# Expert rows of a mixture-of-experts layer: stored and gathered at the end, or added to the output by indirect DMAs

## The reference

```python
# router: 4 groups x 8 experts; each token takes the 2 best of its best group
gate = softmax(top_logit) * g_w[:, None]
flat_e = g_idx[:, None] * 8 + top_idx
# each expert: the tokens that chose it, in blocks padded with a row of zeros
def run_block(xblk, e):
    hid = silu(xblk @ w1[e]) * (xblk @ w3[e])        # 1024 -> 512
    return hid @ w2[e]                               # 512 -> 1024
y[slot_tok] += yb * slot_w[:, None]                  # weighted, two experts a token
out = x + y
```

## Time and profile before

| | us |
|---|---|
| median of 3 runs (1937.62 to 1944.29) | 1937.9 |
| the profiled execution's own time | 1937.75 |
| its span in the trace | 1935.9 |
| PE busy | 1719.5 (89%) |
| PEld busy | 1246.5 (64%) |
| DVE busy | 1138.3 (59%) |
| ACT busy | 893.8 (46%) |
| POOL busy | 796.3 (41%) |

### The profile page before, as it was taken

The page is one execution under the profiler, slowest core; times in us unless marked ns, Lnnn a source line. Parts: engine busy times, 40 slices in busy tenths (PEclk is TensorE's granted clock), DMA queues, the critical chain, the costliest instruction groups (busy, mean ns, idle before and its releaser), DMA issues.

```text
span 1935.9 us, 22760 instructions
## 1 busy us (share of the span) xinstructions
PE 1719.5 (89%) x7364; PEld 1246.5 (64%) x7364; DVE 1138.3 (59%) x1523; ACT 893.8 (46%) x1196; POOL 796.3 (41%) x388
## 2 busy tenths in 40 slices
PE   1888999989999899989689998873999999999993
PEld 1766878777878688458577467662566656666562
DVE  4667865472232346335553314225899998998995
ACT  3534433443224122123321134331888888888882
POOL 0476977333424144104202031100566556665663
PEclk9899999999999899999859999885999999999997
DMA  8344435222242213412104232122999999999995
GB/s 287 115 121 124 129 118 184 88 97 93 76 147 88 109 40 123 165 66 82 67 1 128 87 131 87 44 87 85 337 395 396 393 389 389 396 391 395 389 370 189
DMA packets 138669, 357.94 MB, mean 185 GB/s; under 512 B 12661, under 2 KB 64125, under 8 KB 113768
## 3 DMA queue, kind: packets, MB, share of 16 engines
q1 hardware_dynamic: 130264, 325.32, 46.1%
q10 hardware_dynamic: 4544, 18.88, 2.5%
q0 software_dynamic: 3792, 12.85, 2.1%
HBM read 333.95 MB, written 23.07 MB: 184 GB/s over the span
## 4 chain that ended last, share of the span: by engine, by line
PE 48%; issue 19%; POOL 14%; DVE 11%; DMA 4%; ACT 2%; SPq 1%; POOLq 0%; DVEq 0%; ACTq 0%
PE ps L720 11%; PE ps L721 11%; PE ps L722 11%; PE ps L692 10%; POOL parts L2284 9%; PE ps L702 3%; POOL idx L2294 2%; DMA ring<-in_w_in 1%; DVE act_parts L1671 1%; POOL parts L2250 1%; PE ps L928 1%; PE ps L901 1%; POOL arena L2297 1%; DMA ring<-in_w_out 1%; DMA arena<-in_sgu_b 1%
## 5 line engine op out<-in xcount | busy, mean ns | idle before, releaser
L2250 POOL TENSOR_TENSOR parts<-ring,parts 128x1024 fp32r<-128x1024 f32 x150 | 371.0, 2480 | 808.1 <-ACT parts L1087 805.3
L1366 ACT CAST parts<-ring 128x1024 fp32r<-128x1024 f32 x384 | 396.2, 1048 | 90.9 <-PE ps L722 67.2
L720 PE MATMUL ps<-parts,act_parts 128*128 128x512 f32 (+2 forms) x1088 | 427.8, 393 | 7.1 <-DVE parts L2074 2.2
L721 PE MATMUL ps<-parts,act_parts 128*128 128x512 f32 (+2 forms) x1088 | 423.7, 389 | 0.0
L722 PE MATMUL ps<-parts,act_parts 128*128 128x512 f32 (+2 forms) x1088 | 423.2, 389 | 0.0
L2074 DVE TENSOR_TENSOR parts<-ring,parts 128x1024 fp32r<-128x1024 f32 x289 | 394.3, 1415 | 26.0 <-ACT parts L1366 19.3
L2284 POOL TENSOR_TENSOR parts<-ring,parts 128x1024 fp32r<-128x1024 f32 x95 | 264.1, 2781 | 235.8 <-ACT parts L1366 235.2
L1087 ACT CAST parts<-ring 128x1024 fp32r<-128x1024 f32 x150 | 155.6, 1047 | 409.4 <-PE ps L722 288.5
L720 PE MATMUL ps<-act_parts,parts 128*128 128x512 f32 x640 | 253.9, 397 | 20.4 <-POOL parts L2250 15.6
L721 PE MATMUL ps<-act_parts,parts 128*128 128x512 f32 x640 | 251.0, 392 | 0.0
L722 PE MATMUL ps<-act_parts,parts 128*128 128x512 f32 x640 | 250.9, 392 | 0.0
(11 more groups left out here) (248 smaller groups left out, 1824.3 us busy)
## 6 DMA issues: line engine op xcount, KB each, us to landing
ring<-in_w SPq DMA_DIRECT2D x192, 1024.0 KB, 7.6
ring<-in_w_in SPq DMA_DIRECT2D x30, 1024.0 KB, 7.3
ring<-in_w_in SPq DMA_DIRECT2D x34, 512.0 KB, 5.6
ring<-in_w_ada SPq DMA_DIRECT2D x12, 1024.0 KB, 11.4
ring<-in_w_ret_out SPq DMA_DIRECT2D x8, 1024.0 KB, 10.8
ring<-in_w_out SPq DMA_DIRECT2D x8, 1024.0 KB, 9.7
y_rows<-arena ACTq DMA_DIRECT2D x32, 256.0 KB, 6.4
ring<-in_w_in SPq DMA_DIRECT2D x16, 256.0 KB, 4.0
```

What stands on the lines that cost most here:

```text
L720: pe.matmul(o, lhs[1], rhs[0], start=start, stop=False)
L721: pe.matmul(o, lhs[0], rhs[1], start=False, stop=False)
L1366: act.copy(parts[:, n % 4, 0, :], ring[:, j, n % 4 * 1024:(n % 4 + 1) * 1024]).then_inc(piece_hi, 1)
L2250: pool.tensor_tensor(parts[:, g % 4, 1, :], ring[:, st.place(j), k * 1024:(k + 1) * 1024], parts[:, g % 4, 0, :].bitcast(F32), ALU.subtrac ...
```

## The change

1. **Add in place of store.** `y_blk` is no longer stored by ScalarE. GpSimd adds it to `out` with an indirect DMA that accumulates (`add_to_out`), with the tokens of the block's slots as rows of the destination. `out` is first filled with `x` by one 2 MB store of SP behind that of `h3_rows`. Block c's add has to land (`added`) before GpSimd starts the next turn of the loop and before VectorE may write `y_blk` again (`y_blk_free`).
2. **Weights where the up products meet.** A fifth routing product makes `slot_w`, the weight of each slot, and `hidden` multiplies by it.
3. **Padded slots are skipped.** An empty slot now holds 2048, which is over the bound (511), so gather and add leave its row out. The first slot of a block keeps token 0 when it is empty.
4. **Gone**: the stores to `y_rows`, its clearing, the eight gathers at the end, VectorE's eight operations on them, and the four stores of `out`.
5. **GpSimd's loop** is peeled by one turn, and `add_to_out` and `added` are put into it.

```diff
@@ end of SP's and ScalarE's part
-            sp.wait_ge(zero_ready, 1)
-            ... (4 MB of zeros to the spare rows of y_rows, and the waits on it)
             sp.dma_start(h3_rows.rearrange("(m p) d -> p m d", p=P), h3_tok).then_inc(h3_stored, 16)
+            sp.dma_start(out_v, x).then_inc(out_done, 16)
...
-            for m in range(MT):
-                sp.wait_ge(x_ready, 3 + m + 1)
-                sp.dma_start(out_v[:, m, :], x[:, m, :]).then_inc(out_done, 16)
-            sp.wait_ge(out_done, MT * 16)
+            sp.wait_ge(out_done, 16)
+            sp.wait_ge(y_added, steps * 16 + 16)
+            sp.nop().then_inc(settled, 1)
...
                 up("moe", r + 2, 4, r + 1, ends=("moe", 1, r + 1))
-                store_rows(r)
                 down(r + 1)
@@ TensorE, before its wait for the first gather
+            pe.wait_ge(block_w_ready, 1)
+            filled("route", 4, product(bank("route", 4)[0:SLOTS, 0:64], [slot_oh[:, q, :] for q in range(2 * MT)],
+                                       [block_w[:, q, :] for q in range(2 * MT)]))
@@ VectorE
-            own(dve.tensor_copy(slot_tok[:, :], full("route", 3)[0:SLOTS, 0:64]))
+            o = full("route", 3)[0:SLOTS, 0:64]
+            own(dve.tensor_scalar(slot_tok[:, :], o, float(SKIPPED), None, ALU.add))
+            own.wait()
+            own(dve.tensor_scalar(slot_tok[0:1, :], slot_tok[0:1, :], SKIPPED - 1, None, ALU.bitwise_and))
             own.wait()
             drained("route", 3, dve.nop())
             dve.nop().then_inc(slots_ready, 1)
+            for c in range(2 * MT):
+                own(dve.tensor_scalar(block_w[:, c, :], cst("iota"), blkf[:, c:c + 1], w01[:, c:c + 1], ALU.is_equal, ALU.mult))
+            own.wait()
+            dve.nop().then_inc(block_w_ready, 1)
+            own(dve.tensor_copy(slot_w[0:SLOTS, :], full("route", 4)[0:SLOTS, 0:64]))
...
             def add_rows(c):
-                dve.wait_ge(y_stored, (c + 1) * 16)
+                dve.wait_ge(y_blk_free, c + 1)
...
             def hidden(stage, b, i=0):
-                moe(dve.tensor_tensor(hid[0:SLOTS, :], full(stage, 2, i)[0:SLOTS, :], t_h[0:SLOTS, :], ALU.mult))
+                moe(dve.scalar_tensor_tensor(out=hid[0:SLOTS, :], in0=full(stage, 2, i)[0:SLOTS, :], scalar=w,
+                                             in1=t_h[0:SLOTS, :], op0=ALU.mult, op1=ALU.mult))
@@ GpSimd
-            pool.wait_ge(conv_ready, KT)
-            pool.memset(zeros, 0.0).then_inc(zero_ready, 1)
...
-                pool.indirect_dma_start(xg[0:SLOTS, :], None, h3_rows,
-                                        bass.IndirectOffsetOnAxis(ap=idx[:, 0:1], axis=0)).then_inc(xg_in, 16)
+                pool.indirect_dma_start(xg[0:SLOTS, :], None, h3_rows, bass.IndirectOffsetOnAxis(ap=idx[:, 0:1], axis=0),
+                                        bounds_check=S - 1, oob_is_err=False).then_inc(xg_in, 16)
+
+            def add_to_out(c):
+                pool.wait_ge(y_sum_ready, c + 1)
+                pool.tensor_copy(idx_out[:, :], slot_tok[:, bass.ds(c, 1)]).then_inc(idx_out_ready, 1)
+                pool.wait_ge(idx_out_ready, c + 1)
+                pool.nop().then_inc(settled, 1)
+                pool.indirect_dma_start(out[0], bass.IndirectOffsetOnAxis(ap=idx_out[:, 0:1], axis=0), y_blk[0:SLOTS, :], None,
+                                        bounds_check=S - 1, oob_is_err=False, compute_op=ALU.add).then_inc(y_added, 16)
+
+            def added(c):
+                pool.wait_ge(y_added, (c + 1) * 16)
+                pool.nop().then_inc(y_blk_free, 1)
...
-            with pool.Fori(0, steps) as r:
-                turned("moe", r)
-                gather(r + 2)
-                for n in (3, 7, 11):
-                    low(n, r * 12 + (8 + n))
-            ... (the eight gathers of y_rows)
+            turned("moe", 0)
+            gather(2)
+            for n in (3, 7, 11):
+                low(n, 8 + n)
+            pool.wait_ge(out_done, 16)
+            pool.nop().then_inc(y_blk_free, 1)
+            with pool.Fori(0, pool.snap(steps - 1)) as r:
+                turned("moe", r + 1)
+                gather(r + 3)
+                low(3, r * 12 + 23)
+                add_to_out(r)
+                for n in (7, 11):
+                    low(n, r * 12 + (20 + n))
+                added(r)
+            add_to_out(pool.snap(steps - 1))
+            added(pool.snap(steps - 1))
+            add_to_out(steps)
```

More of the change, by code:

```diff
@@ L25 @@
 NEG = -1e30
+SKIPPED = 2048
 ARENA = 21740
@@ L55, in const_table @@
         ("token", p[:, None] + P * np.arange(MT)[None, :]),
+        ("token_off", p[:, None] + P * np.arange(MT)[None, :] - SKIPPED),
         ("band", band),
@@ L167 @@
     ("xs", 8, 1), ("xpT", 8, 1), ("xo", from_bank(1, 8), 1), ("xout", from_bank(2, 8), 1),
-    ("h3T", KT, 1), ("route", from_bank(1, 4), 1), ("moe0", (0,), 1), ("moe_first", 4, 1),
+    ("h3T", KT, 1), ("route", from_bank(1, 5), 1), ("moe0", (0,), 1), ("moe_first", 4, 1),
     ("moe", 6, 1),
@@ L304, in build @@
         decay = carve([S])
-        zeros = carve([S])
         ln_s = sig_r
@@ L379, in build @@
         taken[0] = expert_free + KT * S
-        combo = carve([4, D])
         y_low = carve([D])
+        block_w = carve([2 * MT, 64])
+        slot_w = carve([64])
         assert taken[0] <= MT * D + 10 * D + 2 * XD + D
@@ L387, in build @@
         idx = sb("idx", [SLOTS, 1], U32)
+        idx_out = sb("idx_out", [SLOTS, 1], U32)
         plan_row = sb("plan_row", [1, P], I32)
@@ L437, in build @@
         y_low_ready, y_sum_ready = sem("y_low_ready"), sem("y_sum_ready")
-        idx_ready, xg_in, xgT_hi, sg_h_ready, hid_ready, hidT_hi, y_blk_ready, y_stored = (sem(n) for n in (
-            "idx_ready", "xg_in", "xgT_hi_ready", "sg_h_ready", "hid_ready", "hidT_hi_ready", "y_blk_ready", "y_stored"))
+        idx_ready, xg_in, xgT_hi, sg_h_ready, hid_ready, hidT_hi, y_added, y_blk_free = (sem(n) for n in (
+            "idx_ready", "xg_in", "xgT_hi_ready", "sg_h_ready", "hid_ready", "hidT_hi_ready", "y_added", "y_blk_free"))
         half_landed = [sem(f"expert_half{n}_landed") for n in range(6)]
@@ L447, in build @@
         conv_stored, conv_back = sem("conv_stored"), sem("conv_back")
-        combo_in = [sem(f"combo{n}_in") for n in range(4)]
+        block_w_ready, slot_w_ready, idx_out_ready = sem("block_w_ready"), sem("slot_w_ready"), sem("idx_out_ready")
         settled = sem("settled")
-        zero_ready, y_cleared = sem("zero_ready"), sem("y_cleared")
-        combo_used, out_done = sem("combo_used"), sem("out_done")
+        out_done = sem("out_done")
         st_ms, st_rms, st_r = mini(0, 32), mini(32, 32), mini(64, 32)
@@ L577, in _ @@
                     head_qk(f"head{h}", 2, h + 1)
-            sp.wait_ge(zero_ready, 1)
-            spare = y_rows[EXPERTS * SLOTS:, :]
-            sp.dma_start(spare.rearrange("r (c d) -> (r c) d", d=S).rearrange("(k p) d -> p k d", p=P),
-                         zeros.unsqueeze(1).to_broadcast([P, spare.shape[0] * D // S // P, S])).then_inc(y_cleared, 16)
             w_ret, w_conv = tiles(a["w_ret_out"][0]), tiles(a["w_conv_out"][0])
@@ L2146, in _ @@
             dve.nop().then_inc(slots_ready, 1)
+            for c in range(2 * MT):
[3 more added lines that the diff above has]
+            own(dve.tensor_copy(slot_w[0:SLOTS, :], full("route", 4)[0:SLOTS, 0:64]))
+            own.wait()
+            drained("route", 4, dve.nop())
             steps = dve.snap(dve.value_load(n_steps[0:1, 0:1], min_val=EXPERTS - 1, max_val=MAX_BLOCKS - 1))
@@ L2180, in hidden @@
             def hidden(stage, b, i=0):
-                moe(dve.tensor_tensor(hid[0:SLOTS, :], full(stage, 2, i)[0:SLOTS, :], t_h[0:SLOTS, :], ALU.mult))
+                w = slot_w[0:SLOTS, b:b + 1] if isinstance(b, int) else slot_w[0:SLOTS, bass.ds(b, 1)]
+                moe(dve.scalar_tensor_tensor(out=hid[0:SLOTS, :], in0=full(stage, 2, i)[0:SLOTS, :], scalar=w,
+                                             in1=t_h[0:SLOTS, :], op0=ALU.mult, op1=ALU.mult))
                 moe.wait()
@@ L2224, in _ @@
             add_rows(steps)
[L2226 to L2236, removed]
         @block.gpsimd
@@ L2308, in _ @@
             low(7, 7)
-            with pool.Fori(0, steps) as r:
-                turned("moe", r)
-                gather(r + 2)
-                for n in (3, 7, 11):
-                    low(n, r * 12 + (8 + n))
-            pool.wait_ge(y_blk_ready, 1)
-            for c in range(2 * MT):
-                q, m = c % 2, c // 2
-                if c >= 4:
-                    pool.wait_ge(combo_used, c - 3)
-                pool.indirect_dma_start(combo[:, c % 4, :], None, y_rows, bass.IndirectOffsetOnAxis(
-                    ap=dest_i[:, 0, q * MT + m:q * MT + m + 1].bitcast(U32), axis=0)).then_inc(combo_in[c % 4], 16)
+            turned("moe", 0)
[15 more added lines that the diff above has]
+            add_to_out(steps)
```

14 lines of the change are left out of this document (1 added, 13 removed).

## The result

| | before | changed |
|---|---|---|
| median of 5 runs, us | 1939.94 (1937.62 to 1944.29) | 1928.12 (1924.30 to 1934.41) |
| profiled execution's own time, us | 1937.75 | 1929.78 |
| its span, us | 1935.9 | 1928.0 |

The ratio is 0.9942, with a 95% interval of 0.9918 to 0.9966: 11.2 us faster (6.6 to 15.9). The forecast was 1928, from a kernel before at 1937.9; with five runs the median before is 1939.94, so 1928 was met with a gain of 11.8 us and not of 10. The next sections show that the total was met with a loop that cost less and an end that brought less than forecast.

The account below looks back on a forecast made before the run. The loop was taken as bound by TensorE plus the latency of GpSimd's slow split. Terms -20.6 (end) + 10.2 (loop) + 0.2 (rest) = -10.2 us on 1937.75 gave 1928 us; own range 1922 to 1936, 8 in 10 1913 to 1968.

Parts of the forecast that it names:

- GpSimd's insert: Expert loop: idx_out copy and add's descriptors ahead of piece 7 make it 0.34 us late, 10 us over 30 turns.
- VectorE has one from 1519.65 here as well: Loop: VectorE's split runs beside the copy of idx_out, so the copy takes 1.17 us and not 0.18.
- The two cases that I gave 0.38 and 0.28: Loop: insert costs 0.15 to 0.6 us a block, landing in time (0.38); rival, insert free, 1917 us (0.28).
- my own sign: Loop: wrong in the main if TensorE's waits for piece 7 don't grow by 0.3 us a block.
- The end: Behind the last add_rows: 26.9 us shrink to 6.3 us, a gain of 20.6 us (18.7 to 22.7).
- the last "0.1" of the sum: End of the span: the final 0.1 us, after the 5.0 us landing, in the sum of 6.3 us.
- The wait `added`: GpSimd's loop, ahead of the next gather: add lands in 8.5 us, within the limit of 9.5, no cost.
- the late landing: Rival, loop: landing from 9.5 us on holds GpSimd in added; 1958 us at 10.5, 2003 at 12; chance 0.28.
- DMA bytes: Expert loop: fewer DMA bytes bring nothing by themselves; rival, loop bound by DMA, about 1909 us, chance 0.06.
- the 0.5 I allowed: Ahead of the loop: the first gather may land up to 0.5 us sooner with half its rows.

Follow-up runs that it names:

- copy_late: Changed kernel with six empty instructions between the wait for y_sum_ready and the copy of idx_out; median 1931.75 us, ratio to before 0.9957.
- copy_early: Changed kernel with the copy of idx_out moved ahead of the wait for y_sum_ready; median 1922.17 us, ratio to before 0.9905.
- add_after_piece7: Changed kernel with add_to_out behind piece 7 in GpSimd's loop, not ahead of it; median 2017.10 us, ratio to before 1.0386.
- plain_write: Changed kernel whose indirect DMA writes the rows and doesn't add them; median 1920.79 us, ratio to before 0.9890.
- gather_all: Changed kernel whose gathers fetch a row for every slot again (token 0 for empty ones), adds still skip; median 1930.34 us, ratio to before 0.9946.

## Why the prediction was right

**The loop: right mechanism, half the turns.** The step said that GpSimd's insert makes piece 7 late by 0.34 us because VectorE's split blocks the index copy (1.17 us). In a slow turn the sum holds: 17.71 - 17.37 = 0.34 us. But "VectorE has one from 1519.65 here as well" was a dead heat, and it went either way: 15 of 30 turns cost next to nothing. The two cases that I gave 0.38 and 0.28 both occurred, in one execution. So 15 x 0.34 = 5.1 us in place of 10.2. (The table has 5.8: quick turns take 17.38 us and not 17.37, and the blocks before the loop took back 0.4 us of the 1.0 us by which the first gather was sooner.) By my own sign I was wrong in the main here, since TensorE's waits for piece 7 grew by 0.13 us a block and not by 0.3; they grow by 0.32 only where every turn is slow, in `copy_late`. That the execution fell between the two cases is luck: by the traces with 25 and 29 slow turns nearly all of the 10.2 could have come.

Inside the term two errors cancelled. Piece 7 starts 9.24 us behind the index copy in a slow turn and 1522.39 - 1513.64 = 8.75 before, so 0.49 us late and not 0.34: the distance from copy to DMA is 0.91 us and not 0.78, and the copy takes 1.27. But the piece is 0.16 us shorter than before (2.88 and 3.04), and only its end counts. The descriptors take 1.50 us and not the 1.11 of a gather, but the next piece starts 1.05 us after the add's start. The wait for the signal was 0.33 us, as read. `copy_late` (all slow, +5.1 us) and `copy_early` (all quick, -4.5 us) show the two sides.

**The end: landing right, an end behind it missed.** The add took 4.6 us to land (5.0 forecast, between 2.9 and 6.9), and signal, copy and distance took 1.4 us (1.2). The failed step is the last "0.1" of the sum: GpSimd is the last engine to issue a DMA, and it needs 5.6 to 6.2 us to leave its program. That sets the end, 2.9 us behind the landing, and the gain is 17.9 and not 20.6 us.

**The wait `added`: right.** The landing was 7.5 us and at most 8.2, against 8.5 taken and a limit of 9.5; the index copy of the gather never waits for a DMA. `add_after_piece7` shows the mechanism of the late landing at work, 4.3 us a block.

By the formula of the Trainium skill ("DMA: Bandwidth & Descriptors", anatomy of one DMA) the add would have landed in an estimated 2.6 us or less; the trace has 4.6 us on idle queues and 7.5 us under load, so the measurement decides again. That a write to HBM can be confirmed surprisingly late (the Trainium skill, "Perfetto Trace Analysis", the notes on the DMA's lifecycle) is hardly seen: the plain write of `plain_write` landed in 3.1 us at the end, and the first gather, a read of HBM, in 2.7.

For the dead heat the Trainium skill has a rule ("SBUF — State Buffer", who interferes with whom, and the summary of rules for kernel authors): a VectorE instruction with two SBUF inputs contends with a GpSimd instruction that reads SBUF, and the second to issue is blocked until the first finishes. The traces agree as far as they resolve it. The copy takes 0.18 us in `copy_early`, where it is over before VectorE's piece starts. Where it is slow it ends with VectorE's instruction, whether it starts together with it (1.27 us) or 0.47 us behind it (0.80 us).

**DMA bytes: right.** 392 became 378 GB/s and the block didn't get shorter; `gather_all` puts the gathered rows back at no cost in the loop. Skipping rows saved GpSimd nothing either: a gather's descriptors take 1.10 us in both.

**Small things.** The first gather came 1.0 us sooner, more than the 0.5 I allowed. The last block took 1.3 us longer, which no step had. VectorE started its last pieces 0.4 us later, which I can't explain. The other 0.9 us are TensorE's last 16 matmuls, some of which ran at the lower of its two clocks, 1.2 GHz (0.43 us each and not 0.23). Before the change TensorE idled 3.8 us and began them at a granted clock of 1.00; the clock fell to 0.50 at about 1902.0, behind the first two matmuls, and held eight. Afterwards TensorE idled 4.2 us, the clock fell while it waited (0.55 from 1909 to 1910, matmuls from 1910.55), and it held twelve. That the total came out at 1928 is luck in part: the loop cost 5 us less and the end brought 3 us less than forecast, and the median of the kernel before, from which the forecast was counted, moved by 2 us.

## What to carry to other kernels

Here a signal released GpSimd's copy just as VectorE, which gave the signal, began its own next instruction. The two shared something, and the copy cost what the race gave it, turn by turn. Put such an instruction ahead of the wait if its inputs are there already. A new DMA on GpSimd is priced by its descriptors (an accumulating one 0.5 us more than a plain one here), by when the next instruction ends and not only by when it starts, and by what stands behind its wait. One that comes last in the program is also priced by the engine's own way out. A total that is met is no proof of its terms: check each against the trace.

## What the runs showed that I had not expected

- An accumulating indirect DMA of 64 rows of 4 KB, half of them skipped, holds GpSimd for 1.50 us against 1.00 for a plain one. The last one of the program lands in 4.6 us against 3.1 (4.0 to 4.7 in five traces), and the median under load in 7.5 against 6.7.
- The DMAs of one loop at 378 GB/s delay an add by 3 us; issued 10.8 and not 3.9 us behind the start of piece 3, in a loop at 318 GB/s, it still lands in 7.9.
- GpSimd needs 5.6 to 6.2 us from its last DMA's descriptors, or from its last wait, to the end of the span.
- A copy of 64 words takes 0.18 us or up to 1.27, by a difference in its start that the trace doesn't resolve (0.01 us or less), and the share of slow ones went from 11 to 29 of 30 between traces with the same loop or nearly the same.
- Piece 7 on GpSimd takes 2.57, 2.88 or 3.04 us for the same work, by what runs beside it.
